# Hybrid trunk on one core: attention's opening work placed between the last projection jobs, output products started per token tile

## What is computed

```python
hx = rms_norm(x, norm1_g) * (1 + sc1) + sh1            # same for the context: hc
ux, vx, bx, cx, zx, qx, kx, vvx = split(hx @ w_in)     # layer 0 also for hc
qx, kx = axial_rope(qx), axial_rope(kx)                # latent tokens only
a = gelu(ux) * (w_s @ rms_norm(gelu(vx)) + b_s)        # gMLP, chunks of 128 tokens
b = bx * conv3(cx * zx)                                # convolution over tokens
c = softmax([q k_local, q k_ctx, sink]) @ [v_local, v_ctx]
x = x + g1 * (concat[a, b, c] @ w_out)
x = x + g2 * moe(rms_norm(x) * (1 + sc2) + sh2)        # 16 experts, top 2
```

## Time and profile before

| what | value |
|---|---|
| median of three runs | 981.01 us (980.45 to 983.00) |
| profiled execution: span of core 0, first to last instruction | 981.6 us (the profile gives no other time of it) |
| mean granted TensorE clock | 0.928 |
| TensorE matmuls busy | 830.5 us, 85% |
| VectorE, ScalarE, GpSimd busy | 406.2 us (41%), 159.5 us (16%), 151.3 us (15%) |
| moved by DMA | 322.56 MB, mean 329 GB/s |
| the chain that ended last: DMA, TensorE, VectorE | 46%, 41%, 7% |

### The profile page before, as it was taken

The page is one execution under the profiler, slowest core; times in us unless marked ns, Lnnn a source line. Parts: engine busy times, 40 slices in busy tenths (PEclk is TensorE's granted clock), DMA queues, the critical chain, the costliest instruction groups (busy, mean ns, idle before and its releaser), DMA issues.

```text
span 981.6 us, 22337 instructions
## 1 busy us (share of the span) xinstructions
PE 830.5 (85%) x8859; PEld 485.7 (49%) x8859; DVE 406.2 (41%) x893; ACT 159.5 (16%) x384; POOL 151.3 (15%) x284
## 2 busy tenths in 40 slices
PE   4699999888996889999896671999887899998674
PEld 2236633555444446657463441587544455654332
DVE  2132722676545423333231124641834655553223
ACT  3201100454013011111010011311512000000001
POOL 2302100001402334433231234000000000000000
PEclk9799999999997799999997886899998899999778
DMA  9999997534998899999999995296076799999995
GB/s 355 348 390 374 349 366 285 230 100 163 382 413 311 338 343 398 391 397 385 384 394 402 399 381 199 89 340 257 1 290 256 293 419 420 420 419 399 418 412 235
DMA packets 82359, 322.56 MB, mean 329 GB/s; under 512 B 10688, under 2 KB 28320, under 8 KB 57712
## 3 DMA queue, kind: packets, MB, share of 16 engines
q1 hardware_dynamic: 62544, 288.42, 75.3%
q0 software_dynamic: 12160, 27.89, 8.0%
q10 hardware_dynamic: 7584, 5.19, 1.8%
HBM read 297.27 MB, written 24.28 MB: 328 GB/s over the span
## 4 chain that ended last, share of the span: by engine, by line
DMA 46%; PE 41%; DVE 7%; issue 3%; ACT 2%; POOL 1%; SPq 0%; DVEq 0%; POOLq 0%; ACTq 0%
DMA weight_ring<-in_w_up_dram 19%; DMA weight_ring<-in_w_gate_dram 18%; PE bank2to L1374 9%; DMA weight_ring<-in_w_mod_dram 5%; PE bank2to L1252 5%; PE bank L1255 4%; PE bank2to L1255 4%; PE bank L1465 4%; PE bank L1252 4%; PE bank2to L1155 2%; DVE score_max L1791 2%; DMA weight_ring<-in_w_in_dram 1%; DMA h_by_expert<-q_k_transposed,slot_numbers 1%; PE bank L1477 1%; PE bank L1327 1%
## 5 line engine op out<-in xcount | busy, mean ns | idle before, releaser
L1465 PE MATMUL bank<-weight_ring,qk_tokens 128*32 128x256 f32 x3824 | 250.9, 406 | 59.5 <-DMA weight_ring<-in_w_up_dram 54.3
L1465 PEld LDWEIGHTS bank<-weight_ring,qk_tokens 128*32 128x32 f32 x3824 | 145.2, 116 | 147.4 <-issue 86.3
L881 POOL DMA_DIRECT2D qk_tokens<-h_by_expert x144 | 71.6, 497 | 161.2 <-DVE qk_tokens L2040 132.3
L1374 PE MATMUL bank2to<-weight_ring 128*128 128x512 f32 x192 | 83.9, 595 | 2.9 <-DVE weight_ring L1819 2.9
L1093 ACT ACTIVATE qk_tokens<-bank 64x256 f32<-64x256 f32 x62 | 23.3, 375 | 374.2 <-PE bank L1465 374.2
L2040 DVE STREAM_TRANSPOSE qk_tokens<-qk_tokens 128x256 f32<-128x256 f32 x36 | 23.6, 655 | 142.6 <-PE bank L1465 132.2
L1477 PE MATMUL bank2to<-weight_ring,qk_tokens 128*32 128x256 f32 x1280 | 79.3, 385 | 1.0 <-DVE qk_tokens L2053 1.0
L818 POOL TENSOR_SCALAR row_stats<-row_stats 128x1 f32<-128x1 f32 x22 | 4.7, 214 | 436.2 <-ACT weight_ring L1136 224.1
L2048 DVE TENSOR_TENSOR qk_tokens<-qk_tokens,bank 64x256 f32<-64x256 f32 x62 | 26.2, 423 | 102.8 <-ACT qk_tokens L1093 101.5
L2053 DVE STREAM_TRANSPOSE qk_tokens<-qk_tokens 64x128 f32<-64x128 f32 x124 | 51.1, 412 | 27.8 <-PE bank2to L1477 26.1
L1477 PEld LDWEIGHTS bank2to<-weight_ring,qk_tokens 128*32 128x32 f32 x1280 | 48.0, 113 | 25.6 <-issue 2.8
(11 more groups left out here) (277 smaller groups left out, 918.3 us busy)
## 6 DMA issues: line engine op xcount, KB each, us to landing
weight_ring<-in_w_down_dram SPq DMA_DIRECT2D x64, 1024.0 KB, 7.6
weight_ring<-in_w_up_dram SPq DMA_DIRECT2D x63, 1024.0 KB, 8.5
weight_ring<-in_w_gate_dram SPq DMA_DIRECT2D x60, 1024.0 KB, 8.4
weight_ring<-in_w_mod_dram SPq DMA_DIRECT2D x24, 2048.0 KB, 10.1
weight_ring<-in_w_in_dram SPq DMA_DIRECT2D x12, 1024.0 KB, 9.1
h_by_expert<-qk_tokens POOLq DMA_DIRECT2D x17, 512.0 KB, 16.4
weight_ring<-in_w_out_dram SPq DMA_DIRECT2D x4, 2048.0 KB, 11.7
y_by_expert<-qk_tokens ACTq DMA_DIRECT2D x158, 32.0 KB, 5.9
```

The lines of the kernel that those rows point to most:

```text
L881: pool.dma_start(hrow[i][q * SLOTS:(q + 1) * SLOTS, :], hsort[bass.ds((n * 2 + (AHEAD + i)) * SLOTS, SLOTS), q * Q:(q + 1) * Q]).then_inc( ...
L1374: mm = pe.matmul(pb[2 + n % 2][:, :], mixt(l)[:, k, t * P:(t + 1) * P], wout(l)[:, hf, k, :], start=(k == 0), stop=(k == KD - 1))
L1465: mm = pe.matmul(gate_bank(l)[32 * g:32 * g + 32, 0:Q].rearrange("p (c f) -> p c f", c=2), hTe[:, k * SLOTS:(k + 1) * SLOTS], w.rearrange( ...
```

## The change

It moves these things, in both layers:

- The jobs' order becomes c, c, z, z, u, u, b, b; the last two (b) go to banks 0 and 1 (`job_bank`, `bank_user`), so that four PSUM banks are free for scores earlier. The weights of u and b change places in memory and in SP's list.
- The transposes of q and k of tile t come right behind job len-7+t (`turned_with`, `turn_qk`), through one pair of banks (6 and 7) instead of two; their copies go to the same places in ScalarE's and VectorE's streams.
- The gMLP products and `score(0)` come behind the third last job, `score(1)` behind the second last; `exps(0)` and `exps(1)` come before the evacuations of the two b jobs.
- On VectorE all of `gmlp`, six of eight convolution steps, `stats(0)` and `stats(1)` and one more step come before the attention loop; one step is left behind pair 0. In layer 0 `partial_sums(4)` and `(5)`, which stood ahead of the copies of the turned keys, now stand behind the sixth convolution step and just before the loop.
- `out_job` waits for its own tile's normalisation, and only before the fifth of its eight k-steps.
- SP loads the second half of `w_out` behind modulation chunk 21, and waits for the finished gMLP (`s_gm` 4) where it waited for the turned tiles.
- `partial(3)` goes to another buffer, and a wait for TensorE before it is gone.

```diff
-            jobs += [("b", j, "A") for j in range(2)] + [("u", j, "A") for j in range(2)]
+            jobs += [("u", j, "A") for j in range(2)] + [("b", j, "A") for j in range(2)]
...
+        def job_bank(l, n):
+            return pb[n % 4 if n < len(proj_jobs(l)) - 2 else n - (len(proj_jobs(l)) - 2)]
+        def turned_with(l, n):
+            t = n - (len(proj_jobs(l)) - 7)
+            return t if 0 <= t < NALL else None
...
         def score_pair(i):
-            a = 512 * (0 if i % 2 else 2)
+            a = 512 * (2 if i % 2 else 0)
...
-                    load_wout(0)
+                    load_wout(0, (0,))
                     load_mod(2 * LATE[0] + 1)
+                    load_wout(0, (1,))
...
-                sp.wait_ge(s_qtp.sem, s_qtp.at(l, NALL))
+                sp.wait_ge(s_gm.sem, s_gm.at(l, 4))
...
-                exps(0)
-                exps(1)
+                for n, (kind, i, eng) in enumerate(J):
+                    if l == 0 and finished(n - 1) is not None:
+                        copy_mod(finished(n - 1))
...
+                    if n == len(J) - 2:
+                        exps(0)
+                    elif n == len(J) - 1:
+                        exps(1)
+                    if eng == "A":
+                        evacuate(n, kind, i)
...
+                    if turned_with(l, n) is not None and turned_with(l, n) < NT[l]:
+                        copy_qT(turned_with(l, n))
...
+                def turn_qk(t):
+                    if t < NX:
+                        pe.wait_ge(s_rope.sem, s_rope.at(l, t + 1))
...
+                    if t >= 1:
+                        pe.wait_ge(s_qtA.sem, s_qtA.at(l, min(t, NT[l])))
+                        pe.wait_ge(s_qtV.sem, s_qtV.at(l, t))
+                    if t < NT[l]:
+                        for b in range(4):
+                            pe.transpose(pb[6][:, b * P:(b + 1) * P], qk[:, t, b * P:(b + 1) * P], ident)
+                    for b in range(2):
+                        mm = pe.transpose(pb[7][:, b * P:(b + 1) * P], qk[:, t, W_C + b * P:W_C + (b + 1) * P], ident)
+                    mm.then_inc(s_qtp.sem, 1)
...
+                def score(i):
...
+                    if i == 0:
+                        pe.wait_ge(s_pV.sem, s_pV.at(l, NALL + 2))
+                    elif l == 0 and i == 1:
+                        pe.wait_ge(s_mr, LATE[0])
...
+                    if turned_with(l, n) is not None:
+                        turn_qk(turned_with(l, n))
+                    if n == len(J) - 3:
+                        gates()
+                        score(0)
+                    elif n == len(J) - 2:
+                        score(1)
-                if l == 0:
-                    pe.wait_ge(s_mr, LATE[0])
...
                 def turn(i):
                     n = keys(S[i][0])[1]
+                    if i == 0:
+                        pe.wait_ge(s_gm.sem, s_gm.at(l, 3))
...
-                pe.wait_ge(s_on.sem, s_on.at(l, NT[l]))
                 pe.wait_ge(s_gm.sem, s_gm.at(l, 4))
                 pe.wait_ge(s_conv.sem, s_conv.at(l, 2))
...
                     for k in range(KD):
+                        if hf == 0 and k == HK:
+                            pe.wait_ge(s_on.sem, s_on.at(l, tiles(l).index(t) + 1))
...
                 for j, n in enumerate(zs):
+                    copy_kT(j)
...
                 if l == 0:
                     add_mod(8)
-                    partial_sums(4)
-                    partial_sums(5)
-                    add_mod(9)
...
+                copy_kT(2)
...
+                for n in (0, 1, 2, 4, 5, 6):
+                    conv_step(n)
+                copy_kT(3)
+                if l == 0:
+                    partial_sums(4)
+                    add_mod(9)
+                gmlp(0)
+                gmlp(1)
                 stats(0)
                 stats(1)
-                gmlp(0)
+                conv_step(3)
+                if l == 0:
+                    partial_sums(5)
                 for i in range(len(S)):
                     copy_pt(i)
-                    if i == 1:
-                        gmlp(1)
...
-                    if i < 8:
-                        conv_step(i)
+                    if i == 0:
+                        conv_step(7)
```

More of the change, by code:

```diff
@@ L610, in load_win, with load_wout @@
                 sp.dma_start(win(l, g), w_in[l, :, c0:c0 + n].rearrange("(k p) n -> p k n", p=P)).then_inc(s_win[g].sem, 16)
-            def load_wout(l):
-                for hf in range(2):
+            def load_wout(l, halves=range(2)):
+                for hf in halves:
                     window.room(2 * MB)
@@ L972, in _, with evacuate @@
                         ins.then_inc(s_hmA, 1)
-                turning = None
-                for n, (kind, i, eng) in enumerate(proj_jobs(l)):
-                    if l == 0 and finished(n - 1) is not None:
-                        copy_mod(finished(n - 1))
-                        turning = finished(n - 1) if turned(finished(n - 1)) else None
-                    if eng != "A":
-                        if turning is not None:
-                            copy_turned(turning)
-                            turning = None
-                        continue
+                def evacuate(n, kind, i):
                     act.wait_ge(s_pj.sem, s_pj.at(l, n + 1))
-                    bank = pb[n % 4]
+                    bank = job_bank(l, n)
                     N = NT[l] * P
@@ new lines, in _ @@
+                S = pairs_of(l)
+                def score(i):
+                    t, b = S[i]
+                    k0, n = keys(t)
+                    if i == 0:
+                        pe.wait_ge(s_pV.sem, s_pV.at(l, NALL + 2))
+                    elif l == 0 and i == 1:
+                        pe.wait_ge(s_mr, LATE[0])
+                    for r in range(2):
+                        a = 64 * r
+                        mm = pe.matmul(score_pair(i)[:, r, 0:n], qT[a:a + 64, b, t * P:(t + 1) * P], kT[a:a + 64, b // 2, k0:k0 + n],
+                                       start=True, stop=True, tile_position=(a, 0))
+                    mm.then_inc(s_sc.sem, 1)
@@ new lines, in gates @@
+                def gates():
+                    pe.wait_ge(s_vn.sem, s_vn.at(l, NT[l]))
+                    pe.wait_ge(s_qtA.sem, s_qtA.at(l, NT[l]))
+                    pe.wait_ge(s_qtV.sem, s_qtV.at(l, NALL))
+                    for j in range(2):
+                        for t in range(NT[l]):
+                            for r in range(2):
+                                h = 2 * j + r
+                                mm = pe.matmul(pb[6 + j][64 * r:64 * r + 64, t * P:(t + 1) * P], vt[:, t, h * 64:(h + 1) * 64], wst[:, h, :],
+                                               start=True, stop=True, tile_position=(0, 64 * r))
+                        mm.then_inc(s_gp.sem, 1)
@@ L1340, in inverse_rows @@
                     mm.then_inc(s_dr.sem, 1)
-                score(0)
-                pe.wait_ge(s_pA.sem, s_pA.at(l, evacuated(J, len(J), "A")))
-                pe.wait_ge(s_pV.sem, s_pV.at(l, evacuated(J, len(J), "V")))
-                score(1)
-                pe.wait_ge(s_vn.sem, s_vn.at(l, NT[l]))
-                for j in range(2):
-                    for t in range(NT[l]):
-                        for r in range(2):
-                            h = 2 * j + r
-                            mm = pe.matmul(pb[j][64 * r:64 * r + 64, t * P:(t + 1) * P], vt[:, t, h * 64:(h + 1) * 64], wst[:, h, :],
-                                           start=True, stop=True, tile_position=(0, 64 * r))
-                    mm.then_inc(s_gp.sem, 1)
                 for i in range(len(S)):
@@ L1739, in _ @@
                     add_mod(8)
[L1740 to L1747 removed]
+                copy_kT(2)
                 def gmlp(j):
                     dve.wait_ge(s_gp.sem, s_gp.at(l, j + 1))
[L1751 to L1752 removed]
+                    dve.wait_ge(s_pA.sem, s_pA.at(l, evacuated(J, len(J) - 3 + j, "A")))
+                    tmp = work(l, 9216, 512)
                     g3 = tmp[:, 0:N].rearrange("p (t q) -> p t q", q=P)
[L1754 removed]
+                    V.scalar_tensor_tensor(out=g3, in0=pb[6 + j][:, 0:N].rearrange("p (t q) -> p t q", q=P),
                                            scalar=mt[:, MT_GMLP + j:MT_GMLP + j + 1], in1=bsb[:, j, :].unsqueeze(1).broadcast_to([P, NT[l], P]),
```

98 lines of the change are left out of this document (38 added, 60 removed).

## The result

| | before | changed |
|---|---|---|
| median, this comparison | 980.90 us (980.45 to 983.00, 4 runs) | 973.15 us (969.71 to 973.37, 4 runs) |
| span of the profiled execution | 981.6 us | 971.0 us |
| granted TensorE clock, mean | 0.928 | 0.924 |

The ratio is 0.9903, 95% interval 0.9884 to 0.9923: 7.8 us by the medians, 7.6 to 11.4 by the interval. The forecast was 971.6 us, 9.4 less than before. In the first of these one execution of the kernel before took 1691.31 us, and the ratio leaves it out.

A forecast was written before the change was run, and what follows sets the result against it. Expert weight loads bound two long stretches, which start earlier when computing ahead ends earlier; attention loops hang on a path between engines. Layer 0's 4.1 us plus layer 1's 5.2, together 9.3 to 9.4, took 981.0 to 971.6 us; range 967 to 977.

The forecast's parts named there:

- The start of the loops: Work ahead of `turn(0)`: waits between moved pieces vanish, winning 1.0 us in layer 0 and 2.3 in layer 1.
- The loops: `turn(0)` to first output job: bound by the path between engines, 48.7 us in layer 0 and 27.7 in layer 1.
- the walk: Attention loops timed instruction by instruction with mean durations; old order gave 51.8 and 31.0 us, new order 48.7 and 27.7.
- mostly `gmlp(1)`: Layer 0's loop: of 3.1 us won, 1.6 are the loop, mostly from removing `gmlp(1)` (0.75 + 0.69).
- `partial_sums(5)`: VectorE directly before layer 0's loop: the moved sum costs nothing; cover 1.2 us, behind which each us is paid.
- Chunk 23: Modulation chunk summed in layer 0's output jobs: margin shrinks from 1.8 to 0.2 us, cost 0, bound 1.6.
- The output jobs: After both loops: the 1.5 us wait for the last normalisation goes; no gap over 0.5 us at `sum_partials`.
- The sum: Whole kernel: 4.1 us from layer 0 and 5.2 from layer 1, together 9.3 to 9.4, giving 971.6 us.
- (1): Load stream from 344: scatter traffic, zeroing and loads hold it in place, layer 0's 4.1 us swallowed, 975.7; chance 0.14.
- (2): Attention loops: all removed VectorE work lay on the path, 4.4 + 3.1 us more won, 964; half, 968, chance 0.09.
- (3): Last projection jobs: TensorE stops at `score(1)` until `add_mod(9)` is through, gain eaten, about 981; chance 0.04.
- (4): Last seven projection jobs of both layers: transposes between them lower TensorE's clock, 993 to 1045 us; chance 0.04.

The follow-up runs named there:

- the first of these: The changed kernel unaltered, run again beside the kernel before in the first experiment session; 971.59 us, ratio 0.9873.
- e3: The changed kernel, but the first output job waits for all tiles' normalisation as before; 976.04 us.
- e4: The changed kernel with the eight convolution steps back behind pairs 0 to 7 of both attention loops; 971.96 us.
- e9: The changed kernel with the first three of four k-steps of `partial_sums(5)` done twice ahead of layer 0's loop; 976.18 us.
- e5: The changed kernel with all of `partial_sums(5)` done twice ahead of layer 0's loop; 975.76 us.
- e8: The changed kernel with the first output job's first four k-steps ahead of the last `turn`, `partial_sums(6)` left whole behind the last normalisation; 973.08 us.
- e6: The changed kernel with SP's loads held back until all tiles but the last are normalised, in both layers; 970.62 us.
- the two others: The changed kernel unaltered, run twice more beside the kernel before in the experiment sessions; ratios 0.9873 and 0.9885.
- e1: The change in layer 0 only, layer 1 mostly in the old order, against the kernel before; 979.01 us, ratio 0.996.
- e2: The change in layer 1 only, layer 0 mostly in the old order, against the kernel before; 973.99 us, ratio 0.9904.
- e7: The changed kernel with the first output job's first four k-steps ahead of the last `turn` and `partial_sums(6)` spread before three normalisations; 970.40 us.
- e10: The changed kernel with four output k-steps ahead of the last `turn` and `partial_sums(6)` spread, run again in another session; 971.66 us.

## Why the prediction was right, and where its sizes were off

**The start of the loops.** Right by mechanism and within 0.3 us. `turn(0)` came at 189.01 in an execution whose chain began 0.35 us later than before's, so at 188.66 for a forecast of 188.7. Layer 1 won 2.06 from its first c job on, where 2.3 was worked out. The old waits that went there are 0.22, 0.24, 0.61 and 0.98 us, 2.05 together. The sum left out 0.28 us that the new order adds: the two jobs behind scores took 3.65 and 3.55 us from start to next start, where undisturbed ones take 3.46.

**The loops.** Right: 48.34 and 27.20 for 48.7 and 27.7. The path between engines binds, not VectorE's sum. Of the gains of 3.55 and 3.43, e3 gives 1.6 each to the output job's wait (1.5 predicted) and e4 gives 1.2 and 0.5 to the convolution. The terms mis-sized were the rest: layer 0's loop gained 1.95 for the 1.6 named, and the removed convolution there was worth 1.2 where the walk gave 0.6. So "mostly `gmlp(1)`" was wrong: by e4 most of it was convolution, and gMLP and all else have some 0.8 us. One step was wrong in kind: the prediction took 0.4 off layer 1's sum because the walk was 0.4 too long in the old order (31.0 for 30.6). It is 0.5 too long in the new order as well (27.7 for 27.2); such an error cancels in the difference, and 3.3 should have stood.

**`partial_sums(5)`.** Its cost of nothing held. The cover is 2.0 us and not 1.2, measured by e9. "Behind which each us is paid" is true for e9 only; in e5 a delay of 2.6 us cost 4.8.

**Chunk 23.** Taken as 0 with a bound of 1.6: 0. Its margin was 0.7 us for 0.2 predicted, and e8 showed that it is real. I had said that SP's early loads cost and gain nothing; e6 agrees for the whole, but with the loads held back to 228 TensorE waited 0.68 us here, which the early loads spare it.

**The output jobs.** No wait and no gap at `sum_partials`, as predicted.

**The sum.** Stages: 10.1 us for 9.3 to 9.4, with layer 1's start taken from the c job. Against the prediction the four parts are 0.06 and 0.45 more in layer 0, 0.25 less and 0.5 more in layer 1. Times: 7.8 in the first comparison, 12.2 and 11.1 in the two others; the stages' sum lies between. That the absolute forecast came so near is in part luck. The profiled span fell to 971.0 where 972.2 was forecast, 1.2 us too little gain. The time was put 0.6 below the span where it is 2.1 above, 2.7 the other way. Together they make the 1.6 us by which the median was missed, which is also about the scatter of the runs. The streams were forecast to start 4 and 9 us earlier and stay as long; by the experts' first products they started 5.5 and 12.5 us earlier, and in this profile the second was 1.9 us longer.

**Rivals.** (1) refuted by e1, whose stream ended 6 us earlier. (2) refuted by the loops themselves, which won 1.95 us in layer 0 and 1.8 in layer 1 of some 6.0 and 4.9 removed, and by e4. (3) did not happen: `score(1)` at 181.41 without a wait, `add_mod(9)` at 172.56 where near 173 was predicted. (4) did not happen through transposes: the clock is 1.00 in both stages and in the projection jobs ahead of them, and groups of two to six transposes between jobs of 16 matmuls left these at 7.0 and 3.5 us. The Trainium skill ("TensorE: Matmul & The Clock Gate", Part 4) would have transposes not count as busy; groups of this length don't bring the clock down here. Where it did come down, in e5 and e8, TensorE had stood still for 3.21 and 2.59 us. The prediction looked for the clock in the wrong part of the change: the place to fear it was a late VectorE ahead of the loop.

**Open.** Why e9's stream in layer 0 took 3.7 us longer, and how much of e2's surplus of some 4 us is more than scatter. Whole times scatter in places that the change doesn't touch. Layer 1's stream took 194.4, 191.7 and 192.0 us from the first expert product in three profiles of the changed kernel. The chain's start in layer 0 lay at 59.91 in e6 and at 62.46 in e7, whose kernels are the same up to there. What the gMLP work cost in the loops is open too.

## What to carry to other kernels

In a loop that alternates between engines, walk the chain with durations from the trace before counting removed work as gain: of some 7 us of convolution only 1.7 counted. Ahead of a long load stream it pays to finish earlier, since the stream moves with its start. And when work is moved to stand just before a loop, compute not only the delay behind its cover but TensorE's whole wait: the waits of 2.59 and 3.21 us here were paid a second time in clock, that of 1.89 us was not. Read gains of 1 us from intervals between fixed points of two profiles (these repeated to 0.05 us inside a stage), not from whole times. Take the fixed point as near to the change as there is one: from the stream's end to layer 1's `turn(0)` the profiles with the new order differ by up to 2.0 us, from the first c job by 0.01.

## What the hardware showed that I had not expected

**The clock after a wait.** Waits of TensorE, the next group's length, and the granted clock behind it: 1.89 us, 0.63 us for four transposes, 1.00 (e9); 2.59 us, 1.89 for 1.04, 0.50 (e8); 3.21 us, 1.09 for 0.63, 0.53 over 6 us (e5). The length of the wait alone does not decide: at the router of layer 0 in the changed kernel, a wait of 1.90 us, with one of 1.57 us 2.9 us before it, was followed by transposes at the lower level (first row below; granted clock 0.75 from 300.5 to 303.0 and 0.50 from 303.4 to 305.4). The engine's work before the waits differed, and no run separates the two. The same loss stands in the kernel before already, behind the output products of layer 1 (granted clock 0.50 from 753 to 756), and in the changed kernel. TensorE and windows of the changed kernel:

```profile
303.47 1.97 PE L1424 MATMUL bank<-consts_sb,q_k_transposed 128*128 128x128 f32 x8 [1.90 <-DVE q_k_transposed L1893]
...
741.12 1.97 PE L1424 MATMUL bank<-consts_sb,q_k_transposed 128*128 128x128 f32 x8 [2.32 <-DVE q_k_transposed L1893]
```

```profile
724.00:735.00 11.00, 11.00 (x29) 4.92 (x28) 3.92 (x5) 1.15 (x2) 0.74 (x2) 1.00 0.36 152
...
741.00:744.00 3.00, 2.21 (x10) 2.10 (x10) 0.93 (x3) 0.59 (x1) 0.00 (x0) 0.50 1.01 427
```

After two waits of 2.33 and 2.32 us the eight transposes take 1.97 us, 1.04 where they come at the full clock (at 734.77). That is a place to look next.

**A load's time depends on what was issued ahead of it.** The same 2 MB of chunk 23 landed 9.6 us after its issue in e7 and 9.5 in e10, 17.0 in the changed kernel and 18.4 in e6. What differs is its place among GpSimd's zeroing writes of 0.5 MB each. In e7 SP issued it at 241.56, 2.1 us ahead of the first of them (243.67). In the changed kernel it was issued at 243.58, with six of them ahead (from 240.78 on). In e6 six of them and the 2 MB of gate weights, issued from 233.33 on, were ahead. In e7 it was the first zeroing write that took longer instead, 7.7 us to landing for 3.1 in the changed kernel.
